# Hybrid decoder block: memory-query tiles in seven-product blocks, table steps packed into fewer tiles, side work and exchanges moved

## The chip, the cores and the metric

The kernel runs on one core of one Trainium2 chip. A core has a matrix engine (TensorE, PE in the rows), VectorE (DVE), ScalarE (ACT), GpSimd (POOL) and SyncE (SP), which here only starts transfers; 16 DMA engines move the data. The metric is the device time of one execution in microseconds (us), the median of several runs. A separate profiled execution gives the trace; all rows below come from it.

## The reference

One layer over x of 2048 tokens by 1024 channels, then a final RMSNorm. It reads, cut to what matters here:

```python
proj = rms_norm(x, norm_g) @ w_in            # 2048 x 8704: 68 tiles of 128 output columns
u_ssm, z_ssm, q, k, v, z_attn, q_mem, z_mem, gate_logits = split(proj)
y = gelu(s5_ssm(u_ssm, ...)); y = y * sigmoid(y @ w_glu + b_glu); o_ssm = y * silu(z_ssm)
o_attn = dilated_attention(q, k, v, rel_bias) * silu(z_attn)       # 12 heads, three dilations
s_mem = einsum(q_mem, k_mem) * MEM_HEAD_DIM ** -0.5                # 4 heads, 256 memory rows
o_mem = softmax(s_mem) @ v_mem * silu(z_mem)
gates = sigmoid(gate_logits + b_gate)
x = x + sum(gates[i] * (o_i @ w_br_i)) @ w_out
```

Everything is float32. The SSM needs tables of powers of a complex number, of sines and cosines, made from 48 groups of parameters. The four tiles of `q_mem` are the memory queries.

## The kernel before

A float32 product is made of three matmuls on rounded parts (`three_pass`, lines 138 to 140): a high and a low part of each factor, so every product of a 128x128 weight with 512 tokens is three matmuls of 128x512.

**Direct stage.** The first `N_Z` = 28 tiles of `w_in` are made directly: `project` (L2752) goes through a tile's four chunks of 512 tokens, each 8 depths x 3 = 24 matmuls, 96 a tile. ScalarE copies a chunk out (`keep_chunk`, L1496); a chunk's bank is written again three chunks later. Six of these tiles (attention values, N_VAL = 6 on) are also turned, chunk by chunk, in the tile after them (PE L2774, DVE L2116). VectorE splits each next tile's weights in two (L130, L132), which waits until TensorE has left the tile that held the buffer.

**Tables.** Between the chunks stand the steps of the SSM tables. There are NU = 12 units of eight steps w = 0..7. `table_step` puts one step behind each chunk from tile N_TAB = 4 on, so a unit takes two tiles. On VectorE w = 0 makes angles of powers (first instruction `sm_ldt`, L1958), w = 1 the matrices (last instruction `ca`, L1980, signal `ca_ready`), w = 3 the transposable part and two angle rows, w = 5 the response (`kpad`, L2086, signal `k_ready`) and two more angle rows, w = 7 a copy. On TensorE w = 4 is four small matmuls that wait for `ca_ready`, and w = 6 four transposes (L2795). On ScalarE w = 0, 3 and 5 are sines, w = 7 the exponential `sm_dt` (L1580) that the next unit's w = 0 waits for. On SyncE w = 6 stores the response in eight transfers (L818), then cosines (L824), then loads the next unit's parameters; the sines of w = 5 wait until those cosines have landed. Each engine works through its own list in order.

**GpSimd** meanwhile adds tiles of h into the operands of the later blocks (`make_operands`, L1250 to L1261) and stores them to `hx_d`: eight sets of four quarters, three sets early and then one quarter a tile up to tile 23.

**Block stage.** The other 40 tiles are made in pairs, two tiles by two chunks of tokens at a time, by seven products of half depth instead of eight (names A11, S2, S4, A12, S3, A22, S1): 7 x 4 depths x 3 = 84 matmuls where the direct way has 96. There are NBK = 40 such blocks. Twice, behind the blocks in `SWAPS` (7 and 27), the seven operands are exchanged: SyncE loads each (1 MB, `load_operand`, L1094) once its last product is made, ScalarE rounds it (`operand_hi`, L1514), VectorE takes the rest (`operand_lo`, L2343), and the next block's product waits for that. `block_at` gives the order: 16 blocks of silu tiles, then the gates.

**Side work.** Into the blocks 8 slots each are spread (`side_slot`): first the SSM's 24 pairs of groups, then from slot `B0` = 128 on the attention, counted in beats, and from beat `M0` the memory attention. Block stage over, the GLU, the branch projections and the output projection follow, which the change does not touch.

Of the kernel before, what the change touches and what calls it, by code (L numbers as in the profile page):

```python
# [42 lines left out]
NU = G // UG  # L43
# [19 lines left out]
def build_program(nc, x_t, mem_t, x_n, mem_n, norm_g, mem_norm_g, final_g, w_in, w_kv, b_gate, ssm_par, ssm_d, w_glu, b_glu,  # L63
                  w_br, w_out, rel_bias, buckets, ident_c, anti_c, sign_c, steps_c, powers_c, y_out):
    ctx = ExitStack()
    with ctx:
# [106 lines left out]
        N_VAL, N_TAB, N_Z, N_GATE = 6, 4, 28, 44  # L173
# [12 lines left out]
        N_SILU = (N_GATE - N_Z) // 2  # L186
        O_SLOT = ((3, 0), (0, 0), (2, 1), (3, 1), (0, 1), (1, 1), (2, 0))
        IN_PLACE = (A11, S4, A12)
        SWAPS = (N_SILU - 1, N_SILU + NPAIRS - 1)
        N_STEPS = NPR * NBK + 3  # L190

        def block_at(b):

            if b < N_SILU:
                pair, ts = b, (3, 2)
            elif b < 2 * N_SILU:
                pair, ts = 2 * N_SILU - 1 - b, (1, 0)
            elif b < N_SILU + NPAIRS:
                pair, ts = b - N_SILU, (1, 0)
            else:  # L200
                pair, ts = NBK - 1 - b + N_SILU, (3, 2)
            return N_Z + 2 * pair, ts
# [110 lines left out]
        def table_step(n, c):  # L313

            u, part = divmod(n - N_TAB, 2)
            return u, 4 * part + c
# [65 lines left out]
        B0 = 128  # L382
        M0 = A_END + 4
# [196 lines left out]
        def bank(b, group):  # L580

            return psum[(b + {"c11": 0, "u": 1, "c21": 2, "c22": 0}[group]) % 3][:, :]
# [46 lines left out]
        LOAD_Y, GELU = (300, 302, 304, 306, 308, 310), (307, 311, 316)  # L629
# [118 lines left out]
        with nc.Block() as block:  # L748
            @block.sync
            def _(sp):  # L750
# [79 lines left out]
                def table_slot(n, c):  # L830
                    u, w = table_step(n, c)
# [8 lines left out]
                    if 0 <= u - 1 < NU - 1 and w == 1:  # L840
                        keep_inputs(u - 1)
                        keep_cosines(u - 1, 1)
# [87 lines left out]

                def load_queries(j):
# [47 lines left out]
                def memory_beat(beat):  # L979
                    if beat == A_END + 3:  # L980
                        sp.wait_ge(o_mm, NT_B)
                        for i in range(2):
                            sp.wait_ge(stored[i], 16 * (N_Z // 2))
                            load_queries(i)
# [172 lines left out]
                for v in range(N_STEPS):  # L1157
                    row, at = divmod(v, NPR)
                    if at == 0 and row + 1 < NBK:
                        load_a11(row + 1)  # L1160
                    if at == 1 and row + 1 < NBK and row + 1 not in AGAIN:
                        load_a12(row + 1)
                    if at == 4 and row + 2 < NBK and row + 2 not in AGAIN:
                        load_a21(row + 2)
                    if at == 6 and row + 2 < NBK and row + 2 not in AGAIN:
                        load_a22(row + 2)
                    if v and product_at(v - 1) is not None and product_at(v - 1)[0] in SWAPS:
                        b, i = product_at(v - 1)
                        sp.wait_ge(*count(mul_done, MADE[v - 1]))
                        load_operand(stage_of(b) + 1, i)  # L1170
                    if (row, at) == (NBK - 1, 3):
# [55 lines left out]
            def _(pool):  # L1227
# [125 lines left out]
                for n in range(2, N_Z):  # L1353
# [72 lines left out]
            def _(act):  # L1426
# [100 lines left out]
                def finish(to, src, b, row):  # L1527

                    kind, tile, _ = TILES[block_at(b)[0] + row]
                    if kind == "silu":  # L1530
# [30 lines left out]
                def table_slot(n, c):  # L1561
                    u, w = table_step(n, c)
# [170 lines left out]
                for v in range(N_STEPS):  # L1733
# [24 lines left out]
                    for swap in SWAPS:  # L1758
                        done = product_at(v - 5) if v >= 5 else None
                        if done is not None and done[0] == swap:  # L1760
                            operand_hi(stage_of(swap) + 1, done[1])
# [93 lines left out]
            def _(dve):  # L1855
# [240 lines left out]
                def table_slot(n, c):  # L2096
                    u, w = table_step(n, c)
# [337 lines left out]
                for v in range(N_STEPS):  # L2435
# [829 lines left out]
```

## Time and profile before

| | |
|---|---|
| median of 3 runs | 2365.92 us (2365.56 to 2367.65) |
| profiled execution, its own time | 2367.38 us |
| its span in the trace | 2365.6 us |
| TensorE busy | 2336.1 us, 99% |
| VectorE / ScalarE / GpSimd busy | 1798.3 (76%) / 790.1 (33%) / 287.7 (12%) us |
| mean granted TensorE clock | 0.996 of full |
| tile 4 starts, direct stage ends | about 135 and 681 us |

Matmuls are pipelined: one's duration in the trace (0.39 us) is longer than the distance to the next one, so what a matmul costs is read from the distance of starts. A busy TensorE says that something was in it, not that it was fast; idle time of another engine costs nothing unless TensorE waits for it. In the views "idle before <-X" names what ended an engine's idle time.

### The profile page before, as it was taken

The numbers are of one execution on the slowest core, as the hardware profiler recorded it, in microseconds if no ns is written. First come the engines' busy times: TensorE is split into PE (matmuls) and PEld (weight loads), VectorE is DVE, ScalarE is ACT, GpSimd is POOL, SyncE is SP. The second block draws the span as 40 slices with busy tenths as digits, with TensorE's granted clock in tenths as the row PEclk, the third lists the DMA queues.
The fourth block names the chain that finished last, engine by engine and source line by source line (L and its number), as shares of the span: only waits on it lengthen the run. The fifth ranks groups of instructions, "written<-read, shape, count | busy, mean of one in ns | idle before, by whom it ended". The sixth has DMA issues, their size and how long they took to land.

```text
span 2365.6 us, 32904 instructions
## 1 busy us (share of the span) xinstructions
PE 2336.1 (99%) x12142; PEld 1894.9 (80%) x12142; DVE 1798.3 (76%) x3225; ACT 790.1 (33%) x1633; POOL 287.7 (12%) x400
## 2 busy tenths in 40 slices
PE   9999999999999999999999999999999999999998
PEld 8888888888887776787777777888888888888887
DVE  7457887787688879867787877788676777786875
ACT  6222212222243334335555575444552011110101
POOL 0421111111001111110000000111100000000000
PEclk9999999999999999999999999999999999999999
DMA  8444354344475577544444474688755866758471
GB/s 336 149 117 132 91 144 144 123 141 131 122 218 180 177 251 222 179 134 169 139 143 134 160 278 148 214 289 274 250 204 181 267 178 186 227 178 246 147 245 54
DMA packets 193811, 431.70 MB, mean 182 GB/s; under 512 B 29295, under 2 KB 74451, under 8 KB 184180
## 3 DMA queue, kind: packets, MB, share of 16 engines
q1 hardware_dynamic: 154036, 273.32, 37.2%
q0 software_dynamic: 38576, 154.19, 19.0%
q8 instruction: 97, 1.59, 0.3%
q10 hardware_dynamic: 1040, 2.10, 0.2%
q14 instruction: 62, 0.51, 0.1%
HBM read 283.38 MB, written 146.11 MB: 182 GB/s over the span
## 4 chain that ended last, share of the span: by engine, by line
PE 94%; DVE 2%; DMA 2%; ACT 1%; issue 1%; SPq 0%; DVEq 0%; ACTq 0%
PE bank L138 28%; PE bank L140 27%; PE bank L139 27%; PE bank L2914 2%; PE bank L2935 1%; PE bank L2957 1%; PE bank L2809 1%; PE bank L2893 1%; PE bank L2823 1%; PE bank L2826 1%; PE bank L2871 1%; DMA w_raw<-w_br 1%; PE bank L2945 1%; DMA sign<-sign_c 1%; DVE h_lo L2343 1%
## 5 line engine op out<-in xcount | busy, mean ns | idle before, releaser
L138 PE MATMUL bank<-h_hi,w_hi 128*128 128x512 f32 (+1 forms) x2320 | 925.3, 399 | 16.0 <-DVE h_lo L2343 13.7
L140 PE MATMUL bank<-h_hi,w_lo 128*128 128x512 f32 (+1 forms) x2320 | 902.7, 389 | 0.0
L139 PE MATMUL bank<-h_lo,w_hi 128*128 128x512 f32 (+1 forms) x2320 | 901.5, 389 | 0.0
L138 PEld LDWEIGHTS bank<-h_hi,w_hi 128*128 128x128 f32 x2320 | 436.5, 188 | 116.5 <-issue 29.5
L140 PEld LDWEIGHTS bank<-h_hi,w_lo 128*128 128x128 f32 x2320 | 436.2, 188 | 92.2
L139 PEld LDWEIGHTS bank<-h_lo,w_hi 128*128 128x128 f32 x2320 | 436.8, 188 | 87.9 <-issue 1.7
L138 PE MATMUL bank<-h_hi 128*128 128x512 f32 (+1 forms) x704 | 270.2, 384 | 2.2 <-issue 1.1
L140 PE MATMUL bank<-h_hi,h_lo 128*128 128x512 f32 (+1 forms) x704 | 264.2, 375 | 0.0
L139 PE MATMUL bank<-h_lo,h_hi 128*128 128x512 f32 (+1 forms) x704 | 264.0, 375 | 0.0
L138 PEld LDWEIGHTS bank<-h_hi 128*128 128x128 f32 x704 | 132.5, 188 | 31.1 <-issue 8.2
L140 PEld LDWEIGHTS bank<-h_hi,h_lo 128*128 128x128 f32 x704 | 132.5, 188 | 24.3
L139 PEld LDWEIGHTS bank<-h_lo,h_hi 128*128 128x128 f32 x704 | 132.7, 188 | 23.9 <-issue 1.0
L1496 ACT ACTIVATE ev<-bank 128x512 f32<-128x512 f32 x112 | 65.3, 595 | 246.6 <-PE bank L140 229.9
L130 DVE CAST w_hi<-w_raw 128x1024 fp32r<-128x1024 f32 (+1 forms) x81 | 63.9, 789 | 102.3 <-PE bank L140 84.2
L1508 ACT ACTIVATE w_hi<-w_raw 128x512 fp32r<-128x512 f32 x129 | 80.7, 629 | 166.4 <-PE bank L140 147.3
L1827 ACT ACTIVATE h_hi<-tb 128x512 fp32r<-128x512 f32 x32 | 20.2, 632 | 343.4 <-DVE tb L2584 343.4
L1596 ACT ACTIVATE tsc<-tsc,stat 128x256 f32<-128x256 f32 (+1 forms) x192 | 88.4, 465 | 57.6 <-DVE stat L2197 57.6
L132 DVE TENSOR_TENSOR w_lo<-w_raw,w_hi 128x1024 fp32r<-128x1024 f32 (+1 forms) x81 | 99.6, 1230 | 2.8
L2194 DVE SCALAR_TENSOR_TENSOR tsc<-bank,bias 128x512 f32<-128x512 f32 x80 | 54.8, 685 | 48.2 <-PE bank L2871 41.5
L2337 DVE TENSOR_TENSOR w_lo<-w_raw,w_hi 128x512 fp32r<-128x512 f32 x129 | 88.1, 683 | 2.6 <-ACT w_hi L1508 2.5
L2574 DVE SCALAR_TENSOR_TENSOR gt<-gt,bank 128x512 f32<-128x512 f32 x96 | 61.0, 682 | 36.6 <-PE bank L140 22.8
L2337 DVE TENSOR_TENSOR w_lo<-keep,w_hi 128x512 fp32r<-128x512 f32 x91 | 62.3, 685 | 32.1 <-ACT w_hi L1508 32.0
(303 smaller groups left out, 2949.9 us busy)
## 6 DMA issues: line engine op xcount, KB each, us to landing
w_raw<-w_in SPq DMA_DIRECT2D x154, 256.0 KB, 4.4
gt<-proj_d POOLq DMA_DIRECT2D x32, 768.0 KB, 7.8
proj_d<-ev POOLq DMA_DIRECT2D x22, 1024.0 KB, 6.4
proj_d<-ev POOLq DMA_DIRECT2D x81, 256.0 KB, 4.7
proj_d<-keep POOLq DMA_DIRECT2D x79, 256.0 KB, 4.5
lo_raw<-hx_d SPq DMA_DIRECT2D x18, 1024.0 KB, 8.0
w_raw<-w_br SPq DMA_DIRECT2D x32, 512.0 KB, 4.5
wx_raw<-w_br SPq DMA_DIRECT2D x32, 512.0 KB, 4.2
```

What stands on the lines that cost most here:

```text
L130: nc.vector.tensor_copy(hi, raw[:, s, 0:kt, :]).then_inc(w_hi_done, 1)
L132: nc.vector.tensor_tensor(lo, raw[:, s, 0:kt, :], hi.bitcast(F32), ALU.subtract).then_inc(w_split[s], 1)
L138: nc.tensor.matmul(out, ah, bh, start=(start and n == 0), stop=False, skip_group_check=onto)
L139: nc.tensor.matmul(out, ah, bl, start=False, stop=False, skip_group_check=onto)
L140: last = nc.tensor.matmul(out, al, bh, start=False, stop=(stop and n == len(pairs) - 1), skip_group_check=onto)
L1496: nc.scalar.activation(dst, src, ACT.Copy).then_inc(evac_done, 1)
L1508: nc.scalar.activation(factor(b, i)[0], factor_raw(b, i), ACT.Copy).then_inc(wh_done[0], 1)
L1596: nc.scalar.activation(e, e, ACT.Exp, bias=stat[:, 0, at:at + 1], scale=-1.0, accum_out=stat[:, 1, at:at + 1]).then_inc(e_done, 1)
L2194: nc.vector.scalar_tensor_tensor(out, sc, -SCALE, bi, ALU.mult, ALU.add).then_inc(s_biased, 1)
L2337: nc.vector.tensor_tensor(lo, factor_raw(b, i), hi.bitcast(F32), ALU.subtract).then_inc(wl_done[0], 1)
L2574: nc.vector.scalar_tensor_tensor(gates[:, 2 - b, :], gates[:, 2 - b, :], 1.0, psum[3 * (n % 2) + b][:, :], ALU.add, ALU.mult).then_inc(b_g ...
L2914: mm = nc.tensor.matmul(out, va[:, kb, HD * half:HD * (half + 1)], e, start=(part == parts[0]), stop=(part == parts[-1]))
```

## The change

Seven parts, told in the order of the diff:

- `N_Z` falls from 28 to 24: the four memory-query tiles (`T_QM`) leave the direct stage and become two pairs more in the block stage, which now has 44 blocks.
- `ORDER` lists the blocks: 8 silu blocks, 8 silu, 12 gates, 2 queries on chunks (1, 0), then 2 queries and 12 gates on (3, 2). Exchanges stand behind blocks 7 and 29.
- `table_steps` starts at tile 3 and puts the first 88 steps (11 units) on 76 chunks, step x behind chunk floor(76x / 88); twelve chunks carry two steps. The last unit has the eight chunks of tiles 22 and 23.
- The attention starts at slot 136 instead of 128, the memory attention 28 beats behind its end instead of 4, so in slot 266; `queries_kept` makes its loads wait for the query blocks' stores. What stands near the end (`LOAD_Y`, `GELU`) moves by 32 slots with it.
- SyncE's list: in an exchange the operand is loaded first, ahead of the weight loads, of which three are moved by a product.
- GpSimd's quarters: two a tile in tiles 4 and 5, then one a tile up to tile 21.
- In an exchange ScalarE's rounding stands behind the slots of one product, ahead of what the next product asks of it, and VectorE's part ahead of the slots instead of behind them.

```diff
@@ -170,7 +170,7 @@
                  + [("copy", T_QM + i, 1) for i in range(4)]
                  + [("silu", t + i, 1) for t, n in ((T_ZS, 6), (T_ZA, 6), (T_ZM, 4)) for i in range(n)]
                  + [("gate", T_G + i, 1) for i in range(24)])
-        N_VAL, N_TAB, N_Z, N_GATE = 6, 4, 28, 44
+        N_VAL, N_TAB, N_Z = 6, 3, 24
 
 
 
@@ -183,22 +183,19 @@
 
         NPR, NBK, NPAIRS = 7, NT - N_Z, (NT - N_Z) // 2
         A11, S2, S4, A12, S3, A22, S1 = range(NPR)
-        N_SILU = (N_GATE - N_Z) // 2
+        N_QM, N_SILU = 2, 8
         O_SLOT = ((3, 0), (0, 0), (2, 1), (3, 1), (0, 1), (1, 1), (2, 0))
         IN_PLACE = (A11, S4, A12)
         SWAPS = (N_SILU - 1, N_SILU + NPAIRS - 1)
+
+        SILU, QUERY, GATE = (range(N_QM, N_QM + N_SILU), range(N_QM), range(N_QM + N_SILU, NPAIRS))
+        ORDER = ([(p, (3, 2)) for p in SILU] + [(p, (1, 0)) for p in (*reversed(SILU), *GATE, *QUERY)]
+                 + [(p, (3, 2)) for p in (*reversed(QUERY), *reversed(GATE))])
         N_STEPS = NPR * NBK + 3
 
         def block_at(b):
 
-            if b < N_SILU:
-                pair, ts = b, (3, 2)
-            elif b < 2 * N_SILU:
-                pair, ts = 2 * N_SILU - 1 - b, (1, 0)
-            elif b < N_SILU + NPAIRS:
-                pair, ts = b - N_SILU, (1, 0)
-            else:
-                pair, ts = NBK - 1 - b + N_SILU, (3, 2)
+            pair, ts = ORDER[b]
             return N_Z + 2 * pair, ts
 
         def step_of(b, i):
@@ -310,10 +307,19 @@
         def count(counter, n):
             return counter[0], counter[1] + n
 
-        def table_step(n, c):
-
-            u, part = divmod(n - N_TAB, 2)
-            return u, 4 * part + c
+        N_FAST = 4 * (N_Z - 2 - N_TAB)
+        FAST_STEPS = 8 * (NU - 1)
+
+        def table_steps(n, c):
+
+            t = 4 * (n - N_TAB) + c
+            if 0 <= t < N_FAST:
+                steps_in = range(-(-t * FAST_STEPS // N_FAST), -(-(t + 1) * FAST_STEPS // N_FAST))
+            elif t >= N_FAST and n < N_Z:
+                steps_in = (FAST_STEPS + t - N_FAST,)
+            else:
+                steps_in = (-1,) if t == -1 else ()
+            return [divmod(x, 8) for x in steps_in]
 
 
         R = 3
@@ -379,8 +385,8 @@
         MSCALE = MD ** -0.5
         MB = L // (2 * P)
         NT_M = MH * MB
-        B0 = 128
-        M0 = A_END + 4
+        B0 = 136
+        M0 = A_END + 28
...
@@ -828,7 +835,10 @@
                     sp.dma_start(mats_d[u][:, :, 0, :], m3[:, :, :]).then_inc(m3_kept, 16)
 
                 def table_slot(n, c):
-                    u, w = table_step(n, c)
+                    for u, w in table_steps(n, c):
+                        table_part(u, w)
+
+                def table_part(u, w):
...
@@ -928,6 +938,14 @@
                             if group_done(p, c) == t + 1:
                                 load_quarter(p + 1, c)
 
+                def queries_kept():
+                    blocks = N_SILU + NPAIRS + N_QM
+                    sp.wait_ge(c11_stored, 16 * blocks)
+                    sp.wait_ge(c21_stored, 16 * blocks)
+                    for i in range(2):
+                        sp.wait_ge(c12_stored[i], 16 * blocks // 2)
+                        sp.wait_ge(*count(c22_stored[i], 16 * blocks // 2))
@@ -977,10 +995,10 @@
                         sp.dma_start(fb[64 * half:64 * half + 64, i, :], src).then_inc(fz_loaded[i], 16)
 
                 def memory_beat(beat):
-                    if beat == A_END + 3:
+                    if beat == M0 - 4:
                         sp.wait_ge(o_mm, NT_B)
+                        queries_kept()
                         for i in range(2):
-                            sp.wait_ge(stored[i], 16 * (N_Z // 2))
                             load_queries(i)
@@ -1156,18 +1174,18 @@
 
                 for v in range(N_STEPS):
                     row, at = divmod(v, NPR)
-                    if at == 0 and row + 1 < NBK:
-                        load_a11(row + 1)
-                    if at == 1 and row + 1 < NBK and row + 1 not in AGAIN:
-                        load_a12(row + 1)
-                    if at == 4 and row + 2 < NBK and row + 2 not in AGAIN:
-                        load_a21(row + 2)
-                    if at == 6 and row + 2 < NBK and row + 2 not in AGAIN:
-                        load_a22(row + 2)
                     if v and product_at(v - 1) is not None and product_at(v - 1)[0] in SWAPS:
                         b, i = product_at(v - 1)
                         sp.wait_ge(*count(mul_done, MADE[v - 1]))
                         load_operand(stage_of(b) + 1, i)
+                    if at == 0 and row + 1 < NBK:
+                        load_a11(row + 1)
+                        if row and row + 1 not in AGAIN:
+                            load_a22(row + 1)
+                    if at == 2 and row + 1 < NBK and row + 1 not in AGAIN:
+                        load_a12(row + 1)
+                    if at == 5 and row + 2 < NBK and row + 2 not in AGAIN:
+                        load_a21(row + 2)
@@ -1363,8 +1381,9 @@
                     if n < 4:
                         for quarter in range(4):
                             make_operands(n - 1, quarter)
-                    elif n < 24:
-                        make_operands(3 + (n - 4) // 4, (n - 4) % 4)
+                    else:
+                        for x in ((2 * n - 8, 2 * n - 7) if n < 6 else (n - 2,) if n < 22 else ()):
+                            make_operands(3 + x // 4, x % 4)
                 store_tile(N_Z - 1)
                 for v in range(N_STEPS):
                     row, at = divmod(v, NPR)
...
@@ -1766,6 +1786,9 @@
                     if product_at(v) is not None:
                         for j in slots_in(v):
                             side_slot(j)
+                    done = product_at(v - 4) if v >= 4 else None
+                    if done is not None and done[0] in SWAPS:
+                        operand_hi(stage_of(done[0]) + 1, done[1])
                 y_high(2)
                 gelu(3)
                 finish_c12(NBK - 1)
...
@@ -2455,6 +2481,9 @@
                         dve.wait_ge(*count(add_done, ADD["c22", NBK - 1]))
                         nc.vector.tensor_tensor(u2(NBK - 1), bank(NBK - 1, "c22"), u2(NBK - 1),
                                                 ALU.add).then_inc(p1_done[0], 1)
+                    done = product_at(v - 5) if v >= 5 else None
+                    if done is not None and done[0] in SWAPS:
+                        operand_lo(stage_of(done[0]) + 1, done[1])
                     if product_at(v) is not None:
                         for j in slots_in(v):
@@ -2480,10 +2509,6 @@
                         operand_lo(0, A22)
                     if v == 2:
                         operand_lo(0, S1)
-                    for swap in SWAPS:
-                        done = product_at(v - 5) if v >= 5 else None
-                        if done is not None and done[0] == swap:
-                            operand_lo(stage_of(swap) + 1, done[1])
```

The same four lines that leave VectorE's list here leave ScalarE's too. `bank` and `finish` only follow the new numbers of the tiles.

On ScalarE, in the direct stage, the rows below are before's from the exponential that lets the ninth unit begin to that unit's first cosines (`ev<-bank` is a chunk copied out, `sm_dt`, `pw` and `cs` are steps w = 7, 0 and 3):

```order
L1580 ACTIVATE sm_dt<-par 128x4 [waits par_loaded]
L1496 ACTIVATE ev<-bank 128x16x32 [waits stored0,mm_done]
L1565 ACTIVATE pw_mag<-pw_t 128x68 [waits pow_ready]
L1566 ACT_TABLE_LOAD
L1566 ACTIVATE pw_sin<-pw_x 128x68
L1567 ACTIVATE pw_cos<-pw_x 128x68
L1496 ACTIVATE ev<-bank 128x16x32 [waits mm_done] x3
L1575 ACTIVATE cs<-tx 128x256 [waits cs_kept0,ang_ready]
```

In the change, for the eighth unit:

```order
L1604 ACTIVATE sm_dt<-par 128x4 [waits par_loaded]
L1515 ACTIVATE ev<-bank 128x512 [waits stored1,mm_done]
L1589 ACTIVATE pw_mag<-pw_t 128x68 [waits pow_ready]
L1590 ACT_TABLE_LOAD
L1590 ACTIVATE pw_sin<-pw_x 128x68
L1591 ACTIVATE pw_cos<-pw_x 128x68
L1515 ACTIVATE ev<-bank 128x512 [waits mm_done] x2
L1599 ACTIVATE cs<-tx 128x256 [waits cs_kept0,ang_ready]
```

What moved: two chunks instead of three stand between the powers and the cosines; over a whole packed unit it is seven instead of eight (six in the first).

On VectorE, at the first exchange (between blocks 7 and 8), before, the first operand's low part `h_lo<-lo_raw` stands behind the group scan (`tv`, `wv`, `zv`) and a weight's low part:

```order
L2362 TENSOR_TENSOR ev<-bank,keep 128x512
L2132 TENSOR_TENSOR tv<-bank,csb 128x512 x2
L2134 TENSOR_TENSOR wv<-tv 128x256
L2135 TENSOR_TENSOR wv<-tv 128x256
L2140 SCALAR_TENSOR_TENSOR zv<-m8b,wv 128x256 x2
L2337 TENSOR_TENSOR w_lo<-w_raw,w_hi 128x512
L2343 TENSOR_TENSOR h_lo<-lo_raw,h_hi 128x1024 x2
L2374 TENSOR_TENSOR keep<-bank,ev 128x512
```
In the change it stands ahead of them:

```order
L2388 TENSOR_TENSOR ev<-bank,keep 128x512
L2369 TENSOR_TENSOR h_lo<-lo_raw,h_hi 128x1024 x2
L2158 TENSOR_TENSOR tv<-bank,csb 128x512 x2
L2160 TENSOR_TENSOR wv<-tv 128x256
L2161 TENSOR_TENSOR wv<-tv 128x256
L2166 SCALAR_TENSOR_TENSOR zv<-m8b,wv 128x256 x2
L2363 TENSOR_TENSOR w_lo<-w_raw,w_hi 128x512
L2400 TENSOR_TENSOR keep<-bank,ev 128x512
```
What moved: the operand's low part went up past the scan of one pair of groups, four rows of it, and past one `w_lo`.

On SyncE's queue at the same exchange, before, loads of operands (`lo_raw`) and of weights (`w_raw`) alternate:

```order
L892 DMA bias_t<-bt 128x1024
L1064 DMA w_raw<-w_in 128x512
L1094 DMA lo_raw<-hx_d 128x2048
L1064 DMA w_raw<-w_in 128x512
L1094 DMA lo_raw<-hx_d 128x2048
L1064 DMA w_raw<-w_in 128x512
```
In the change the operands come first:

```order
L902 DMA bias_t<-bt 128x1024
L1112 DMA lo_raw<-hx_d 128x2048 x2
L1082 DMA w_raw<-w_in 128x512 x2
L874 DMA ub<-proj_d 128x1x256
```
What moved: two operands go ahead of the weight loads and their waits.

## Rows read from the trace of the kernel before

**Rows 1.** The page's first part: busy us (share), instructions of TensorE.
```profile
PE 2336.1 (99%) x12142; PEld 1894.9 (80%) x12142; DVE 1798.3 (76%) x3225; ACT 790.1 (33%) x1633; POOL 287.7 (12%) x400
```

**Rows 2.** Waits of TensorE over the span: total us, times, longest.
```profile
PE bank L138 <- DVE h_lo L2343: 13.7, 5, 5.7
```

**Rows 3.** Timeline, TensorE: start us, duration us, line, operation. Matmuls twelve apart.
```profile
866.83 0.39 PE L138 MATMUL bank<-h_hi,w_hi 128*128 128x512 f32 x1
869.54 0.39 PE L138 MATMUL bank<-h_hi,w_hi 128*128 128x512 f32 x1
```

**Rows 4.** Timeline, TensorE: the turning step (w = 6) of two neighbouring units, twice.
```profile
267.71 0.49 PE L2795 MATMUL bank<-ident,ba 128*128 128x128 f32 x3
316.09 0.60 PE L2795 MATMUL bank<-ident,ba 128*128 128x128 f32 x4
...
452.28 0.60 PE L2795 MATMUL bank<-ident,ba 128*128 128x128 f32 x4
496.86 0.38 PE L2795 MATMUL bank<-ident,ba 128*128 128x128 f32 x2
```

**Rows 5.** Timeline, VectorE, one unit while GpSimd adds; idle us, releaser in brackets.
```profile
374.36 0.15 DVE L1958 TENSOR_TENSOR sm_ldt<-par,sm_dt 128x4 f32<-128x4 f32 x1
...
402.99 0.21 DVE L2086 TENSOR_TENSOR kpad<-kpad,dpar 16x64 f32<-16x64 f32 x1
...
413.92 0.69 DVE L130 CAST w_hi<-w_raw 128x1024 fp32r<-128x1024 f32 x1 [4.60 <-PE bank L140]
...
418.92 0.15 DVE L1958 TENSOR_TENSOR sm_ldt<-par,sm_dt 128x4 f32<-128x4 f32 x1
```

**Rows 6.** Timeline, VectorE, a unit when GpSimd no longer adds.
```profile
595.20 0.16 DVE L1958 TENSOR_TENSOR sm_ldt<-par,sm_dt 128x4 f32<-128x4 f32 x1
...
611.02 0.76 DVE L1980 TENSOR_TENSOR ca<-ca,tmp 128x576 f32<-128x576 f32 x1
...
621.58 0.21 DVE L2086 TENSOR_TENSOR kpad<-kpad,dpar 16x64 f32<-16x64 f32 x1
```

**Rows 7.** Timeline, SyncE's queue, then ScalarE, the same unit's second half.
```profile
621.83 6.00 SPq L818 DMA_DIRECT2D mats_d<-kpad  x8
...
630.35 0.42 ACT L1575 ACTIVATE cs<-tx 128x256 f32<-128x256 f32 x1 [4.37 <-DMA cs_d<-cs]
...
631.61 0.58 ACT L1496 ACTIVATE ev<-bank 128x512 f32<-128x512 f32 x1
...
637.38 1.28 ACT L1580 ACT_TABLE_LOAD   x1
638.67 0.21 ACT L1580 ACTIVATE sm_dt<-par 128x4 f32<-128x4 f32 x1
```

**Rows 8.** Timeline, VectorE and GpSimd at one moment, then GpSimd in tile 3.
```profile
392.43 1.91 DVE L1980 TENSOR_TENSOR ba<-ba,tmp 128x512 f32<-128x512 f32 x1
...
392.47 1.30 POOL L1259 TENSOR_TENSOR hx<-hx 128x512 f32<-128x512 f32 x1
...
118.02 5.04 POOL L1250 TENSOR_TENSOR hx<-h_hi,h_lo 128x512 f32<-128x512 f32 x4 [3.44 <-DMA hx_d<-hx]
```

**Rows 9.** Groups by line, VectorE, 190 to 650 us: busy, mean ns, idle before.
```profile
L2116 DVE COPY ev<-bank 128x512 f32<-128x512 f32 x24 | 16.1, 688 | 15.5 <-PE bank L2774 15.4
```

**Rows 10.** Windows: us; busy us (count) of PE, PEld, DVE, ACT, POOL; clock; DMA.
```profile
896.00:900.00 4.00, 0.69 (x4) 0.57 (x4) 3.87 (x6) 0.80 (x2) 1.17 (x2) 0.97 1.07 231
900.00:904.00 4.00, 4.00 (x13) 3.17 (x12) 4.00 (x6) 2.85 (x4) 0.57 (x1) 0.60 0.99 387
1416.00:1420.00 4.00, 0.27 (x1) 0.30 (x2) 3.47 (x4) 4.00 (x6) 0.55 (x1) 0.82 1.01 421
1420.00:1424.00 4.00, 4.00 (x26) 2.96 (x27) 3.87 (x6) 2.96 (x4) 0.00 (x0) 0.50 0.43 178
```

**Rows 11.** Timeline, SyncE's queue, first exchange.
```profile
880.90 0.33 SPq L1064 DMA_DIRECT2D w_raw<-w_in  x1
881.27 1.63 SPq L1094 DMA_DIRECT2D lo_raw<-hx_d  x1
```

More of the change, by code:

```diff
@@ L580, in bank @@
         def bank(b, group):
-            return psum[(b + {"c11": 0, "u": 1, "c21": 2, "c22": 0}[group]) % 3][:, :]
+            first = unit(N_Z - 1, 2) - 8
+            return psum[(b + first + {"c11": 0, "u": 1, "c21": 2, "c22": 0}[group]) % 3][:, :]
         def last_product(b, i):
@@ L628, in build_program @@
         N_FIRST = len(FIRST)
-        LOAD_Y, GELU = (300, 302, 304, 306, 308, 310), (307, 311, 316)
+        LOAD_Y, GELU = (332, 334, 336, 338, 340, 342), (339, 343, 348)
         WARM = (22, 6)
@@ L839, in table_slot @@
                                 load_par(u + 1)
-                    if 0 <= u - 1 < NU - 1 and w == 1:
-                        keep_inputs(u - 1)
-                        keep_cosines(u - 1, 1)
+                        if u and w == 1:
+                            keep_inputs(u - 1)
+                            keep_cosines(u - 1, 1)
                 def tables_over():
@@ L1529, in finish @@
                     kind, tile, _ = TILES[block_at(b)[0] + row]
+                    if kind == "copy":
+                        return nc.scalar.activation(to, src, ACT.Copy)
                     if kind == "silu":
@@ L1561, in table_slot, with table_part @@
                 def table_slot(n, c):
-                    u, w = table_step(n, c)
+                    for u, w in table_steps(n, c):
+                        table_part(u, w)
+                def table_part(u, w):
                     if 0 <= u < NU and w == 0:
@@ L1757, in _ @@
                         operand_hi(0, S1)
-                    for swap in SWAPS:
-                        done = product_at(v - 5) if v >= 5 else None
-                        if done is not None and done[0] == swap:
-                            operand_hi(stage_of(swap) + 1, done[1])
                     if (row, at) == (NBK - 1, 5):
@@ L2096, in table_slot, with table_part @@
                 def table_slot(n, c):
-                    u, w = table_step(n, c)
+                    for u, w in table_steps(n, c):
+                        table_part(u, w)
+                def table_part(u, w):
                     if 0 <= u < NU:
@@ L2482, in _ @@
                         operand_lo(0, S1)
-                    for swap in SWAPS:
-                        done = product_at(v - 5) if v >= 5 else None
-                        if done is not None and done[0] == swap:
-                            operand_lo(stage_of(swap) + 1, done[1])
                 split_glu(0, GLU_FREE[0])
@@ L2778, in table_slot, with table_part @@
                 def table_slot(n, c):
-                    u, w = table_step(n, c)
+                    for u, w in table_steps(n, c):
+                        table_part(u, w)
+                def table_part(u, w):
                     if not 0 <= u < NU:
```

## The prediction

> **What bounds the kernel now.** I read the page's first part, then TensorE's waits, then the direct stage engine by engine. TensorE is busy 99% of the span [rows 1], and what it waits for is nearly one thing: the low parts of exchanged operands, 13.7 us in five waits [rows 2]. Everything else is the distance of matmuls: twelve take 869.54 - 866.83 = 2.71 us, so 0.226 us each [rows 3]; the 0.39 us of a row overlaps its neighbours. So a matmul taken away is worth 0.226 us, as long as nothing else becomes late. What could is found in the direct stage. There a table unit passes every 496.86 - 452.28 = 44.6 us where no values are turned and every 316.09 - 267.71 = 48.4 us where they are [rows 4]; VectorE keeps up with only 4.6 us of waiting for TensorE left in a unit [rows 5]. The change shortens that unit.
>
> **Products.** Four tiles leave the direct stage: 4 x 96 = 384 matmuls. Four blocks are added: 4 x 84 = 336. That is 48 fewer, 48 x 0.226 = 10.9 us. It is on the path, since TensorE has no other idle time. By the Trainium skill (TensorE: Matmul & The Clock Gate, Back-to-back issue gap), which gives N / 2.4 + 2.5 ns for a warm matmul, one of 512 columns would be 216 ns and the gain 10.4 us; the trace has 226, and the sum goes by the trace. The small matmuls of tables, scan and attention stay as many.
>
> **Tables, TensorE's side.** 88 steps on 76 chunks make a unit 76/11 = 6.9 chunks instead of 8. From 44.6 us for 8 chunks: a chunk is 24 x 0.226 = 5.44 us, the eight 43.5, so a unit's own small matmuls cost 1.1. The packed unit asks 6.9 x 5.44 + 1.1 = 38.7 us of TensorE; turning values adds (48.4 - 44.6)/8 = 0.48 us a chunk, so 42.0 us there.
>
> **Tables, the loop through the other engines.** A unit cannot follow the last one faster than its own chain. From the first instruction to the end of the response: 621.8 - 595.2 = 26.6 us, one split of weights in it and none of GpSimd's sums [rows 6]. While GpSimd adds it is 403.2 - 374.4 = 28.8 [rows 5]: a two-input sum on VectorE that meets one on GpSimd takes 1.91 us, [rows 8], where a wider sum takes 0.76 when GpSimd is quiet [rows 6]. Then SyncE issues the eight stores of the response, 6.0 us, and the cosines behind them; ScalarE's next sine starts at 630.35, 8.6 us behind the response's end, and the four sines end at 631.6, 1.3 us more. Then ScalarE copies out two chunks that have queued up (0.6 us each), loads its table and makes `sm_dt`: 638.88 - 637.38 = 1.5 us [rows 7]. Only then may the next unit's first VectorE instruction start. Together 26.6 + 8.6 + 1.3 + 1.2 + 1.5 = 39.2 us, with GpSimd's sums in it 41.5, and some 1.8 us more where VectorE also copies values (0.69 us each, three or so in that part [rows 9]): 43.3. Before, 44.6 and 48.4 us covered all of it; after, 38.7 and 42.0 do not.
>
> Which sums meet which part matters. The quarters of GpSimd's work come one a tile, 22 us apart, and the response ends 28.8 us after the unit's start, so there is one or two in the exposed part of each; those behind the response cost nothing. I count one in each. By the skill (SBUF, Who interferes with whom) a GpSimd operation holds the shared port for its whole length; taken as all of a quarter's two 1.3 us sums it would be 2.6 instead of 2.2 us a unit, 4 us more in all.
>
> Sum over the stage. Unit 0 starts about 3 us after tile 3 does and meets eight of GpSimd's sums at once, 118.0 on [rows 8]: 8 x 1.3 = 10.4 us, of which one quarter's worth is counted already and part falls in a wait for ScalarE; I add 4 us. Then ten unit periods until unit 10 starts, of which 3.5 with values: 3.5 x 43.3 + 6.5 x 41.5 = 421.3. So it starts 428.3 us after tile 3. Its step w = 4 on TensorE must wait for `ca_ready`, 611.8 - 595.2 = 16.6 us later [rows 6] plus 2.2 for GpSimd, then 0.5 of its own, three chunks, 16.3, and the turning, 0.6: tile 22 starts at 428.3 + 36.2 = 464.5. TensorE alone needs 19 tiles x 21.75 + 24 x 0.48 + 11 x 1.1 = 436.9. **It waits 28 us**, in pieces of 2 to 6 us, before w = 4 and, where ScalarE is held by the sines, for a chunk to be copied out. In the last two tiles the pace is the old one. Bounds: with GpSimd's sums all in covered places the ten periods are 10 x 39.2, plus 3 for copies: tile 22 starts at 3 + 395 + 34 = 432, before TensorE's own 437, so the stall is the first unit's, about 4 us. With two quarters in a third of the units, and a chunk copy that waits for a late store of values, it is 36. I take 28, since the period of 41.5 is built of measured pieces. What waits behind the waiting w = 4 is all of TensorE's list.
>
> **Exchanges.** They cost 13.7 us of waiting and the clock behind it: granted 0.60 in 900 to 904 us, 0.82 and 0.50 in 1416 to 1424 [rows 10], after TensorE had stood still for 3 us or more. Lost: 4 x 0.40 + 4 x 0.68 = 4.3 us. Together 18.0, nearly 8 at the first, 10 at the second. The second falls at present into the last attention batches, with queries' and keys' loads between the operands'; afterwards its loads meet only the attention's last beats and its conversions none, and I take all but 1 us as gone. The first keeps the group scan beside it; VectorE is busy 3.87 and 4.00 of 4 us there [rows 10], so order alone cannot free it. But the operand load at 881.27 came right behind a weight load at 880.90 that had held SyncE's queue [rows 11], and VectorE's and ScalarE's parts move ahead of waits and scan. I take 6 of 8 as gone: 15 us in all. Bounds 3 (only the attention's overlap matters, in part) and 18.
>
> **At nothing.** The shift of attention and memory attention moves work between blocks whose TensorE time does not depend on it: the slots hold the same matmuls. The first queries' loads wait for the stores of block 31; from slot 262 to 266 there are 14 triples x 0.68 = 9.5 us, for the rest of a store and a 256 KB load. If that cover is short, up to 3 us. Half-speed clock after waits in the direct stage is not counted, since there the loop and not TensorE sets the pace.
>
> **Sum:** -10.9 + 28 - 15 = +2.1 us on the span of 2365.6. The profiled execution itself took 2367.38, the median of the runs is 1.5 lower, 2365.92; on that 2368.0 us.
>
> **Rivals.**
> 1. *The tables stay hidden.* Copies and sums fall into the waits for ScalarE, and the loop is 39 us or less. For it: 39.2 without them is within 0.5 us of the 38.7 asked; VectorE still waits 4.6 us of a unit for TensorE [rows 5]. Against: 28.8 against 26.6 us in the unit's first part. Time: 2365.9 - 10.9 + 4 - 15 = 2344.
> 2. *Half hidden*, one quarter in two exposed: stall 15, 2355.
> 3. *Slower: the first exchange stays as it is and the second keeps half.* One mechanism: an exchange moves 7 MB through the same DMA engines, which are full in 896 to 904 us (share 1.07, 0.99) [rows 10], so an operand is late whatever the order. It decides if landing takes more than the 16 us between the same product in two blocks. With the loop at 28: 2365.9 - 10.9 + 28 - 3 = 2380.
> That the queries' blocks are not worth their matmuls is excluded by rows 3.
>
> **How the numbers follow.** Forecast 0.45 (own range 2358 to 2378), rival 1 0.22, rival 2 0.13, rival 3 0.20. A run tells 0.2%, 4.7 us, from no change. Faster: rivals 1 and 2 and 0.05 of the forecast, 0.40. Within: 0.27, all of the forecast. Slower: rival 3 and 0.13 of the forecast, 0.33. The range leaves out the far ends of rivals 1 and 3: 2343 to 2382.
>
> **What would show it.** Right: TensorE waiting for the line of `ca` (VectorE) in the direct stage, 2 to 6 us a time, 20 us or more in all; the distance of turning steps 41 to 43 us instead of 38.7 or 42.0; VectorE idle less for TensorE, more for ScalarE; the last block product later than TensorE's own count. Waits for the operands' low parts 3 us or less, none near the second exchange, clock 1.0 there. Wrong: turning steps 38.7 us apart with no waits would make rival 1; waits for operands of 8 us or more rival 3.

## The result and the profile after

The changed kernel takes 2392.24 us (median of 4 runs, 2390.98 to 2394.42) against 2366.45 us for the kernel before in the same runs: ratio 1.0109, 95% interval 1.0097 to 1.0122. It is **25.8 us slower**. The forecast was 2368.0 us, with a range up to 2382, so the time lies outside. The profiled span is 2389.0 us against 2365.6.

The page's first part, answering to [rows 1], then TensorE's waits in the changed kernel, answering to [rows 2] (line, what it waited for: total us, times, longest):

```profile
PE 2336.2 (98%) x12094; PEld 1891.4 (79%) x12094; DVE 1838.1 (77%) x3281; ACT 805.5 (34%) x1663; POOL 289.3 (12%) x412
```
```profile
PE bank L2815 <- DVE ca L2003: 26.5, 6, 7.1
PE bank L138 <- DVE h_lo L2369: 6.0, 3, 3.9
PE bank L2799 <- ACT ev L1515: 2.2, 2, 1.2
```

There are 48 fewer matmuls and TensorE is busy for as long as before: it ran slower somewhere. The waits for exchanged operands fell from 13.7 to 6.0 us, and the waits for `ca`, which were none, are 26.5. The last turning step of the direct stage shows in one number what the stage cost. Timelines (start us, us, line, operation), of the kernel before and of the changed one:

```profile
675.21 0.60 PE L2795 MATMUL bank<-ident,ba 128*128 128x128 f32 x4
```
```profile
629.09 0.60 PE L2823 MATMUL bank<-ident,ba 128*128 128x128 f32 x4
```

Both stand at the same distance from the stage's end (the third chunk of its last tile). Four tiles fewer are 384 x 0.2262 = 86.9 us by the distance in [rows 3], so without any loss it would stand at 588.3 us. It stands at 629.1: **the direct stage lost 40.8 us**. In the experiments this marker tells the stage from the rest; it is read from one profiled execution, and in e7, whose direct stage is the change's own, it stands 2.9 us later, so a difference of 3 us in it says nothing.

Half speed is in those 40.8 us. Windows around the second wait in the changed kernel (columns as in [rows 10]):

```profile
180.00:184.00 4.00, 0.80 (x4) 0.33 (x2) 3.50 (x15) 0.00 (x0) 0.00 (x0) 0.91 1.01 385
184.00:188.00 4.00, 0.13 (x4) 0.13 (x8) 3.86 (x6) 0.00 (x0) 0.00 (x0) 0.50 0.20 74
188.00:192.00 4.00, 4.00 (x16) 2.83 (x12) 3.90 (x6) 0.00 (x0) 0.00 (x0) 0.50 0.71 183
192.00:196.00 4.00, 4.00 (x16) 3.25 (x15) 3.66 (x13) 0.72 (x2) 0.00 (x0) 0.81 0.57 80
```

TensorE stood still for 7.1 us, until 187.87. The clock is granted 0.50 in the end of that wait and in the four us after it, and 0.81 in the next four: the lower level, 1.2 GHz, is paid after the wait as well.

What made `ca` late stands some us before such a wait. Timelines of VectorE and of GpSimd in unit 1 of the changed kernel:

```profile
171.89 0.23 DVE L1981 TENSOR_TENSOR pw_ai<-pw_mag,pw_sin 128x68 f32<-128x68 f32 x1
172.16 1.66 DVE L1985 TENSOR_SCALAR pw_sar<-pw_ar,sign 128x68 f32<-128x68 f32 x1
173.85 1.33 DVE L1985 TENSOR_SCALAR pw_sai<-pw_ai,sign 128x68 f32<-128x68 f32 x1
175.21 1.33 DVE L1985 TENSOR_SCALAR pw_nai<-pw_ai 128x68 f32<-128x68 f32 x1
176.58 1.50 DVE L2037 COPY m<-pw_mag 64x2 f32<-64x2 f32 x2
178.11 0.16 DVE L1981 TENSOR_TENSOR sm_den<-par 128x4 f32<-128x4 f32 x1
```
```profile
172.45 1.30 POOL L1272 TENSOR_TENSOR hx<-hx 128x512 f32<-128x512 f32 x1
173.84 1.29 POOL L1274 TENSOR_TENSOR hx<-hx 128x512 f32<-128x512 f32 x1
175.21 1.29 POOL L1277 TENSOR_TENSOR hx<-hx 128x512 f32<-128x512 f32 x1
176.57 1.28 POOL L1279 TENSOR_TENSOR hx<-hx 128x512 f32<-128x512 f32 x1
```

Each small VectorE instruction ends when GpSimd's sum ends, one after another: VectorE advances by one instruction for each sum of 1.3 us. With the sums made short (e5, below) the same instructions take this:

```profile
159.82 0.28 DVE L1987 TENSOR_SCALAR pw_sar<-pw_ar,sign 128x68 f32<-128x68 f32 x1
160.14 0.27 DVE L1987 TENSOR_SCALAR pw_sai<-pw_ai,sign 128x68 f32<-128x68 f32 x1
160.44 0.23 DVE L1987 TENSOR_SCALAR pw_nai<-pw_ai 128x68 f32<-128x68 f32 x1
160.71 0.41 DVE L2039 COPY m<-pw_mag 64x2 f32<-64x2 f32 x2
```

5.8 us have become 1.2. This is what [rows 8] shows in the kernel before, for one wide sum, at one moment.

### The profile page after: what moved, and what is told of

Read it like the earlier page. It is cut to its first block, busy times and chain, and to the rows that moved or that the text cites. A ratio compares the mean times of both kernels' runs of the same rounds, so it can differ in the third digit from the quotient of the medians.

```text
span 2389.0 us, 33026 instructions
## 1 busy us (share of the span) xinstructions
PE 2336.2 (98%) x12094; PEld 1891.4 (79%) x12094; DVE 1838.1 (77%) x3281; ACT 805.5 (34%) x1663; POOL 289.3 (12%) x412
## 4 chain that ended last, share of the span: by engine, by line
PE 76%; DVE 14%; DMA 3%; issue 2%; ACT 2%; SPq 2%; DVEq 0%; ACTq 0%
PE bank L138 22%; PE bank L140 22%; PE bank L139 22%; PE bank L2942 2%; DVE tmp L1981 1%; PE bank L2963 1%; PE bank L2985 1%; SPq L825 1%; PE bank L2851 1%; PE bank L2854 1%; PE bank L2921 1%; PE bank L2837 1%; PE bank L2899 1%; DVE h_lo L2369 1%; DVE sm_t L1981 1%
## 5 line engine op out<-in xcount | busy, mean ns | idle before, releaser
L138 PE MATMUL bank<-h_hi,w_hi 128*128 128x512 f32 (+1 forms) x2280 | 913.5, 401 | 9.2 <-DVE h_lo L2369 6.0
L140 PE MATMUL bank<-h_hi,w_lo 128*128 128x512 f32 (+1 forms) x2280 | 889.9, 390 | 0.0
L139 PE MATMUL bank<-h_lo,w_hi 128*128 128x512 f32 (+1 forms) x2280 | 889.0, 390 | 0.0
L138 PE MATMUL bank<-h_hi 128*128 128x512 f32 (+1 forms) x728 | 279.5, 384 | 2.5 <-issue 1.3
L140 PE MATMUL bank<-h_hi,h_lo 128*128 128x512 f32 (+1 forms) x728 | 273.5, 376 | 0.0
L139 PE MATMUL bank<-h_lo,h_hi 128*128 128x512 f32 (+1 forms) x728 | 273.4, 376 | 0.0
L1599 ACT ACTIVATE cs<-tx 128x256 f32<-128x256 f32 x48 | 20.0, 417 | 261.8 <-DVE tx L1997 150.2
L2363 DVE TENSOR_TENSOR w_lo<-w_raw,w_hi 128x512 fp32r<-128x512 f32 x142 | 97.1, 684 | 6.8 <-ACT w_hi L1527 6.8
L1515 ACT ACTIVATE ev<-bank 128x512 f32<-128x512 f32 x96 | 54.6, 591 | 132.8 <-PE bank L140 115.7
L130 DVE CAST w_hi<-w_raw 128x1024 fp32r<-128x1024 f32 (+1 forms) x77 | 55.4, 719 | 52.9 <-PE bank L140 36.9
```

Of the source, the lines that this page charges most:

```text
L130: nc.vector.tensor_copy(hi, raw[:, s, 0:kt, :]).then_inc(w_hi_done, 1)
L138: nc.tensor.matmul(out, ah, bh, start=(start and n == 0), stop=False, skip_group_check=onto)
L139: nc.tensor.matmul(out, ah, bl, start=False, stop=False, skip_group_check=onto)
L140: last = nc.tensor.matmul(out, al, bh, start=False, stop=(stop and n == len(pairs) - 1), skip_group_check=onto)
L1515: nc.scalar.activation(dst, src, ACT.Copy).then_inc(evac_done, 1)
L2363: nc.vector.tensor_tensor(lo, factor_raw(b, i), hi.bitcast(F32), ALU.subtract).then_inc(wl_done[0], 1)
```

## The experiments

Ratios are against the kernel before on the same chip. "Last turn" is the marker above; "ca" is TensorE's waiting for `ca`. In e3 and e14 the last turn stands three tiles from the kernel before's, so without loss it would be at 675.2 - 65.1 = 610.1.

| kernel | us | ratio (95%) | last turn | ca |
|---|---|---|---|---|
| the change | 2392.2 | 1.0109 (1.0097, 1.0122) | 629.1 | 26.5 |
| e1 cosines first | 2375.5 | 1.0039 (1.0023, 1.0054) | 612.7 | 17.1 |
| e2 before + order | 2366.8 | 1.0001 (0.9993, 1.0010) | - | - |
| e3 before + packing | 2399.8 | 1.0139 (1.0125, 1.0153) | 641.2 | 20.7 |
| e4 filled waits | 2386.2 | 1.0081 (1.0068, 1.0095) | 623.7 | 3.8 |
| e5 short sums | 2356.6 | 0.9954 (0.9941, 0.9968) | 594.3 | 3.4 |
| e6 short sums, cosines | 2353.0 | 0.9941 (0.9928, 0.9955) | 590.3 | 2.4 |
| e7 old order | 2394.5 | 1.0115 (1.0100, 1.0131) | 632.0 | 27.1 |
| e8 even tables | 2375.6 | 1.0039 (1.0027, 1.0052) | 614.3 | 20.5 |
| e9 sums in gaps | 2383.1 | 1.0060 (1.0048, 1.0073) | 617.8 | 9.6 |
| e10 the same, cosines | 2380.6 | 1.0056 (1.0043, 1.0070) | 618.1 | 10.9 |
| e11 gaps behind stores | 2361.3 | 0.9978 (0.9969, 0.9987) | 597.7 | 5.1 |
| **e12** the same, cosines | **2354.0** | 0.9944 (0.9932, 0.9957) | 589.9 | 3.0 |
| e13 before, short sums | 2367.7 | 1.0001 (0.9992, 1.0011) | 674.2 | - |
| e14 e3, short sums | 2370.1 | 1.0007 (0.9998, 1.0017) | 612.3 | 2.8 |

**e1, SyncE's step turned round.**
```diff
                         if w == 6:
-                            keep_response(u)
-                            keep_cosines(u, 0)
                             if u + 1 < NU:
                                 load_par(u + 1)
+                            keep_cosines(u, 0)
+                            keep_response(u)
```


> The changed kernel with SyncE's step w = 6 turned round: the next unit's parameters and the cosines are issued before the eight stores of the response (5.1 us on SyncE). Theory (the loop runs through SyncE): the second half's sines start about 4 us earlier in each unit, the loop falls below the 38.7 us that TensorE asks, the 26.5 us of waits for ca shrink to under 8 and the half clock behind them goes too: 2392 - 25 to 38 = 2354 to 2367 us. Rival (VectorE and GpSimd on one port are the limit, SyncE is beside it): waits for ca stay above 18 us, 2384 us or more.


16.8 us came back, less than the theory asked, and 17.1 us of waits for `ca` stayed, just under the rival's 18. The second half's sines start 4 us sooner (from 36 to 38 us to 32 to 34 us behind a unit's start in most units), but from unit 1 to unit 10 a unit became only 1.2 us shorter (42.8 to 41.6). The ten periods from unit 0's first VectorE instruction to unit 10's fell from 435.0 to 421.7 us, most of the 16.4 us in the marker. SyncE is a part of the loop: starting the sines sooner makes up for a part of what lengthens it, here and less so in e6.

**e2, the exchange's order alone, in the kernel before** (the hunks of the change for SyncE, ScalarE and VectorE).


> The kernel before with the exchange's reorder alone (SyncE: operand first, factor loads later; ScalarE: rounding after the slots at v - 4; VectorE: low part before the slots). Prediction's step: -15 us, 2351. What the two traces give for the exchanges inside the whole change: -9, 2357. Rival (an exchange is bound by its transfers, order does nothing): within 3 us of before, 2364 or more.


Nothing, as the rival had it, though not for its reason. TensorE's waits in e2:
```profile
PE bank L138 <- DVE h_lo L2342: 5.7, 2, 3.9
PE bank L2891 <- ACT tsc L1596: 5.7, 2, 3.5
PE bank L2933 <- DMA qm<-proj_d: 1.8, 1, 1.8
```
The operands are waited for 8.0 us less, and instead the attention beats that lie beside the second exchange wait 7.5 us for ScalarE and for queries. The order passed the lateness on.

**e3, the packing alone, in the kernel before** (`table_steps` in place of `table_step`, 88 steps on 76 chunks from tile 4 on).


> The kernel before with the tables packed alone: 88 steps on 76 chunks from tile 4, still 28 direct tiles, exchanges as before. Theory (the packed unit is shorter than the loop, and each wait is followed by half clock): +30 to +40 us, 2396 to 2406, with waits for ca of 20 us or more. The prediction's step as written: +28, 2394. Rival (the packing is harmless and the loss comes from the attention's shift or the queries' blocks): within 5 us of before.


+32 us, as the theory had it, waits for `ca` and half clock included. By the marker, 641.2 - 610.1 = 31.1 us, the packing alone makes three quarters of the 40.8. Most of the rest goes with the start in tile 3, among the eight sums there: the first two unit periods are 50.0 and 45.9 us in the change, 42.0 and 43.7 in e3. That difference was not isolated.

**e4, waits filled.**
```diff
                         if u:
                             pe.wait_ge(k_out, UG * u)
+                        for _ in range(FILL.get(u, 0)):
+                            nc.tensor.matmul(psum[7][:, P:4 * P], h_hi[:, 0, 0, 0:P], h_hi[:, 0, 0, P:4 * P],
+                                             start=True, stop=True)
+                        pe.wait_ge(ca_ready, u + 1)
```


> The changed kernel with filler products of 384 columns on TensorE ahead of its wait for ca, in the six units that waited (20, 36, 36, 16, 4, 16 of them; their results are not read), so that TensorE does not stand still before w = 4. Theory (the half clock behind a wait is lost on top of the wait): granted clock 1.0 through the direct stage, time falls by 6 to 10 us, to 2382 to 2386. Rival, the prediction's own sentence (the loop sets the pace, so the clock costs nothing): the waits grow by what the clock gives back, 2389 to 2393.


-6 us in the time and 629.1 - 623.7 = 5.4 in the marker, with the clock at 1.00 where it had been 0.50. The same windows in e4:
```profile
184.00:188.00 4.00, 4.00 (x31) 3.64 (x29) 3.86 (x6) 0.00 (x0) 0.00 (x0) 1.00 0.00 0
188.00:192.00 4.00, 4.00 (x25) 3.25 (x18) 3.83 (x8) 0.00 (x0) 0.00 (x0) 1.00 1.05 244
```
So the prediction's sentence, that half speed costs nothing here, is refuted. It costs some 5 us; the intervals of the two times do not overlap. It is not the larger part. The clock is not at 1.00 all through e4's direct stage: it is 0.50 for some three us at 164 and at 249 us, so e4 does not take the whole of it back.

**e5 and e6, GpSimd's sums short.** Over 8 columns from tile 3 on, so the operands of the third set and later are left out; e6 has e1's edit too.
```diff
+                    w = slice(0, CW if q < 2 else 8)
...
-                        nc.gpsimd.tensor_tensor(t3, b22, t1, ALU.subtract).then_inc(hx_sum[0], 1)
+                        nc.gpsimd.tensor_tensor(t3[:, w], b22[:, w], t1[:, w], ALU.subtract).then_inc(hx_sum[0], 1)
```


> The changed kernel with GpSimd's sums from tile 3 on made over 8 columns instead of 512 (the operands from the third on are thus left out; order, stores and semaphores stay). Theory (GpSimd's sums beside VectorE lengthen the loop by 2 us or so a unit, more in units 0 and 1): VectorE's first part of a unit falls from 28 to 31 us to 26 to 28, the waits for ca from 26.5 to 10 us or less, time 2392 - 15 to 25 = 2367 to 2377. Rival (contention is small change, the loop is long by its own instructions and by SyncE): waits stay above 18 us, 2384 or more.

> The same with SyncE's step w = 6 turned round as well. If the loop of SyncE and the sums are all that is late, TensorE waits under 4 us in the direct stage and the clock stays 1.0: 2392 - 38 = 2354, plus or minus 3. If VectorE's own queue (splits and copies, which wait for TensorE, between the tables' instructions) is a third cause: 2360 to 2368.


This is the decisive one: -36 us, more than the theory's 15 to 25, with every store, table and semaphore in place. From unit 0's first VectorE instruction to unit 10's there are 435.0 us in the change and 403.4 in e5, and TensorE asks 10 x 38.7 + 3.5 x 3.3 = 399. The marker is 6.0 us from its ideal, and in e6 2.0, so the third cause that e6's expectation names is not needed. With the sums gone the turn of e1 is worth 4 us by the marker, with them 16: the shares of the two overlap, since each shortens the same loop.

**e7, the change without its exchange order** (e2's hunks taken out).


> The changed kernel with the exchange's order put back on SyncE, ScalarE and VectorE; blocks, spacing of attention and tables stay as changed. If the order is worth nothing, as it was alone in the kernel before, and the gain of 9 us in the exchanges comes from memory attention's no longer lying beside the second one: within 3 us of the change, 2389 to 2395. If order and spacing are needed together: 2398 to 2403.


Its interval overlaps the change's almost whole, so the times show no worth of the order here either. The trace shows what they can't: TensorE waits longer for operands than in the change (6.0) and less than in the kernel before (13.7).
```profile
PE bank L138 <- DVE h_lo L2370: 9.7, 7, 3.3
```
3.3 of these 9.7 us lie at the second exchange, where the change has 2.1 and the kernel before 7.4.

**e8, tables spread evenly from tile 2 on**, with e1's edit.


> A candidate: the changed kernel with step w = 6 on SyncE turned round and the 96 steps spread evenly over the 86 chunks from tile 2, chunk 2, on, 7.17 chunks a unit instead of 6.9 and then 8. TensorE then asks 7.17 x 5.44 + 1.1 = 40.1 us a unit, 43.5 with values. Theory (the loop stands at 40 to 42 us after the turn): waits for ca under 8 us, 2355 to 2364. Rival (waits come from single units that GpSimd or values lengthen, and the mean does not matter): 2370 or more.


No faster than e1. Unit 0, now in tile 2, meets the sums there, and TensorE waits 11.0 us for it. As the rival had it, more room in the mean doesn't help against sums that meet single units.

**e9 and e10, sums tied to VectorE.** e10 has e1's edit too.
```diff
-                    else:
-                        for x in ((2 * n - 8, 2 * n - 7) if n < 6 else (n - 2,) if n < 22 else ()):
-                            make_operands(3 + x // 4, x % 4)
+                    for u in range(10):
+                        if n == N_TAB + (8 * u + 5) * N_FAST // FAST_STEPS // 4:
+                            pool.wait_ge(ang_ready, UG * (u + 1))
+                            for x in (2 * u, 2 * u + 1):
+                                make_operands(3 + x // 4, x % 4)
```


> A candidate that leaves nothing out: the changed kernel with GpSimd's last twenty quarters tied to VectorE. Two quarters (5.1 us of sums) start in each of units 0 to 9 when VectorE has made the unit's last angle (ang_ready), just before it waits for ScalarE's sines, instead of behind the store of a tile. Theory (the sums cost what they meet, 36 us with the clock): most of them now meet VectorE's wait, the waits for ca fall to 10 us or less, 2360 to 2372; units 0 and 1 keep the sums of tile 3. Rival (the sums cost VectorE the same wherever they lie): 2385 or more.

> The same with SyncE's step w = 6 turned round. That shortens the very wait in which the sums now lie. If the two gains add: 2355 to 2362. If the turn takes the room from the sums: no faster than e9 by more than 3 us.


The waits for `ca` fell to 9.6 us as expected, but the time only by 9 us, outside either forecast. Timelines of e9, GpSimd, ScalarE and TensorE:
```profile
371.95 0.99 POOL L1281 DMA_DIRECT2D hx_d<-hx  x1 [0.30 <-POOL hx L1279]
372.94 0.57 POOL L1255 DMA_DIRECT2D v_d<-ev  x1
```
```profile
385.01 0.60 ACT L1517 ACTIVATE ev<-bank 128x512 f32<-128x512 f32 x1 [16.31 <-DMA v_d<-ev]
```
```profile
385.66 0.80 PE L138 MATMUL bank<-h_hi,w_hi 128*128 128x512 f32 x1 [9.35 <-ACT ev L1517]
```
The wait that I added stood in GpSimd's list ahead of the store of the values. The store came at 372.94, ScalarE waited for its landing, TensorE for ScalarE. That is a cost of my edit, not of the sums. e10 is 2.5 us faster than e9, so its second forecast held; it has the same two waits for ScalarE (13.1 us, 12.7 in e9).

**e11 and e12, the wait moved behind the store.**
```diff
-                        for quarter in range(4):
+                        for quarter in range(4 if n == 2 else 2):
                             make_operands(n - 1, quarter)
+                    for u in range(11):
+                        if n == N_TAB + ((8 * u + 5) * N_FAST // FAST_STEPS + 2) // 4:
+                            pool.wait_ge(ang_ready, UG * (u + 1))
+                            for x in (2 * u + 2, 2 * u + 3):
+                                make_operands(2 + x // 4, x % 4)
```


> The candidate of e9 mended at the two places where its trace shows loss: the gate stands half a tile later in GpSimd's list, behind the tile's store (in e9 it held back the store of the values, for which ScalarE and then TensorE waited 9.3 us), and of the eight sums in tile 3 only four stay, the rest go into the gap of unit 0; all twelve tiles of operands are made. Theory: no wait for ScalarE's copies over 3 us, VectorE's excess in the stage below 27 us, waits for ca under 8 us, 2358 to 2366, faster than before. Rival: the sums pushed behind the stores meet the next unit's chain, 2372 or more.

> The same with SyncE's step w = 6 turned round. In e10 the sines began 4 us earlier and the next unit no sooner; so within 3 us of e11.


e11 does what was expected. e12 does not stay within 3 us of it: the turn, worth nothing in e10, is worth 7 us here. The likely reason, not isolated, is that the waits for the values' stores, which set the pace in e10, are gone. **e12, all of the work in it, is 12.1 us faster than the kernel before and 38 us faster than the change.** Its last turning step:
```profile
589.92 0.60 PE L2825 MATMUL bank<-ident,ba 128*128 128x128 f32 x4
```

**e13 and e14, short sums in the kernel before, without and with the packing.**


> The kernel before with GpSimd's sums from tile 3 on made over 8 columns (the operands from the third on left out). Its trace has the same contention: VectorE's instructions are 46.5 us longer between 137 and 600 us than their usual durations. Theory (it was there before and lay hidden under the 44.6 and 48.4 us of a unit): within 3 us of before, 2363 to 2369. Rival (it already cost time, so the change only kept it): 5 us or more faster.

> The packed tables in the kernel before (e3, 2399.8) with the short sums. Theory (all that the packing cost, 32 us, is the contention that it uncovers, with the half clock behind the waits): back to 2364 to 2371. Rival (SyncE's stores and the values' copies hold a part of it): 2375 or more.


Both leave out the same operands as e5. With e3 they make a square: before 2368.1, short sums 2367.7, packing 2399.8, both 2370.1. The sums cost 0 us in the old spacing and 30 us in the packed one; the packing costs 32 us with the sums and 2 without them.

## Why the prediction was wrong

- **Products, -10.9 us: held, as far as the sum shows it.** 48 matmuls are gone; no run has them alone. The sum closes with it: -10.9 + 40.8 in the direct stage - 7.7 at the exchanges = +22.2, against 23.4 in the spans.
- **Where TensorE would wait: held.** At w = 4 for `ca`, 26.5 us in six waits (foreseen 2 to 6 us each, measured 0.7 to 7.1), and 2.2 us for a late copy of ScalarE.
- **The price of the direct stage, +28 us: this step failed.** It was 40.8, outside the bounds of 4 and 36. Two terms of it were mis-sized. First GpSimd's sums, which I took at one quarter, 2.2 us, in the exposed part of a unit, "those behind the response cost nothing". By the trace VectorE's instructions between 115 and 600 us are some 50 us longer than their usual durations (for each shape the difference to its lower quartile, summed over all single instructions), 1 to 2 us in e5. That is nearly 5 us in a unit for two quarters. Sums behind the response delay the angles and splits that the next unit stands behind, and the eight in tile 3, counted as one quarter and 4 us, put the end of unit 0's response at 38.4 us instead of the 26.7 of e5. Ten unit periods took 435.0 us against the 425.3 of the sum (421.3 and the 4 for unit 0), and from unit 10's start to tile 22's it was 39.2 us against 36.2. Without the sums (e5) 6.0 of the 40.8 us are left, near the prediction's own lower bound of 4 for that case. Second the half clock, which I left out "since there the loop and not TensorE sets the pace". e4 shows some 5 us. In unit 6 TensorE waits for VectorE, runs on at half speed, and then VectorE waits for TensorE:
```profile
402.57 0.41 PE L2815 MATMUL bank<-ca,bb 128*16 128x128 f32 x4 [7.03 <-DVE ca L2003]
```
```profile
422.93 0.69 DVE L130 CAST w_hi<-w_raw 128x1024 fp32r<-128x1024 f32 x1 [4.41 <-PE bank L140]
```
  In e4 this wait of VectorE is 1.6 us. So neither engine alone sets the pace, and what the clock loses is not all given back.
- **The shared port.** The Trainium skill (SBUF — State Buffer, Who interferes with whom) says that VectorE and GpSimd share one pair of ports, and that where a VectorE instruction in a two-port mode meets GpSimd, the one that issued first holds the pair for its whole length and the other is fully blocked. The trace agrees that one waits for the other, 1.33 us against 0.27 for the same instruction; in which mode the instruction ran it does not show. I had given the rule only 4 us, by applying it to one quarter a unit.
- **Exchanges, -15 us: half of it.** Waits for operands 13.7 to 6.0 us; the clock's loss, by windows of 40 us around both exchanges, 5.2 us before and 5.2 after (granted 0.96 and 0.91, then 0.91 and 0.96). So -7.7. By exchange, waits and clock together: the first cost 7.9 us before and 7.5 after, where I had taken 6 of 8 as gone; the second cost 11.0 and 3.7. The gain is all at the second, and there e7 has it without the new order (3.3 us). So the order, which was my reason at the first, bought nothing that the times show (e2, e7). At the first exchange VectorE is busy 19.7 of the 20 us from 836 to 856, as it was in [rows 10], and has no room for the low parts:
```profile
853.65 0.77 PE L138 MATMUL bank<-h_hi,w_hi 128*128 128x512 f32 x1 [3.91 <-DVE h_lo L2369]
```
  That the gain at the second comes from attention no longer lying beside it was not isolated from the new order of blocks, since the attention's shift doesn't fit into the kernel before.
- **Rivals.** The first, that copies and sums fall into waits and the tables stay hidden, is what e12 makes of the kernel: it forecast 2344, and e12 takes 2354. With half of the exchanges' gain the sum for e12 is 2365.9 - 10.9 + 1.6 - 7.7 = 2349; the other 5 us stay open. The slower rival, 2380, named the exchanges, and it was the sums.

## What to carry to other kernels

An operation that lengthens another engine's instructions may be free only because there is slack, and its price appears when another edit takes the slack: the sums cost 0 us in the kernel before and 30 in the packed one. To find such a price, run the kernel once with the suspected operation cut to a few columns, before and after, and read the square of four times. Count every such operation in the loop, not only those in the part that looks exposed. When a wait is put on an engine to place its work, put it behind that engine's stores.

## What the runs showed of the hardware

- VectorE's small instructions (128 x 68, 0.23 to 0.28 us) beside GpSimd's two-input sums of 512 columns took 1.33 to 1.66 us, in step with the sums. In the direct stage of the change GpSimd made 64 us of sums and VectorE's instructions were some 50 us longer for them.
- After TensorE had stood still for 3.5 to 7 us in the change, the granted clock was 0.50 for the next 3 to 6 us of running. A wait of 2.2 us at the first exchange was followed by 0.50 in e3, e7 and e14, and not in the kernel before and e13. With 128 more products, laid into those waits, e4 ran 6 us faster.
